# First attention of a two-block network: its four groups spread over four key/value projections instead of one group per projection

## The reference, cut to what matters

```python
def diff_attention(q1, q2, k1, k2, v, lam, bias_dist):     # per block of 128 queries
    def probs(q, k):
        s = einsum('bqhd,bkhd->bhqk', q, k) * scale + bias # q, k: 4 heads x 64
        s = where(causal, s, -inf)
        return softmax(s, axis=-1)
    a = probs(qa, k1) - lam * probs(qc, k2)
    return einsum('bhqk,bkhd->bqhd', a, v)                 # v: 4 heads x 128
...
    o = rms_norm(o, subln_g) * (1.0 - lambda_init)         # per head, over 128
    return concatenate([o, y], axis=-1) @ w_out
```

## Time and profile before

| | |
|---|---|
| median of 3 runs | 1134.58 us (1132.84 to 1136.03) |
| the profiled execution: its time | 1133.13 us |
| its span, first to last instruction | 1131.3 us |
| mean granted TensorE clock | 0.994 |
| PE matmul busy | 1099.1 us, 97% of the span |
| DVE / ACT / POOL busy | 701.5 / 517.9 / 65.0 us |
| HBM read | 222.95 MB, 198 GB/s over the span |

### The profile page before, as it was taken

How to read it: one execution, slowest core, us unless ns; L and a number is a source line. 1 busy time by engine, 2 the same in 40 slices (tenths; PEclk the granted TensorE clock), 3 DMA queues, 4 the chain that set the end, 5 groups by cost and what they waited for, 6 DMA issues and landing times.

```text
span 1131.3 us, 15644 instructions
## 1 busy us (share of the span) xinstructions
PE 1099.1 (97%) x6758; PEld 982.4 (87%) x6758; DVE 701.5 (62%) x666; ACT 517.9 (46%) x584; POOL 65.0 (6%) x116
## 2 busy tenths in 40 slices
PE   6998899999999999999999999999999998999998
PEld 4987689899989898998988898998788887898997
DVE  4655546468675767656645767668757467555544
ACT  5553544454344344333544544444655364453441
POOL 2200000010000000000001000000211010000000
PEclk9999899999999999999999999999999999999999
DMA  9834426264867756455535777586244463655531
GB/s 361 334 118 149 146 96 239 95 211 181 319 222 265 275 206 259 170 188 180 205 112 176 265 284 272 211 326 236 82 149 168 167 224 130 214 189 192 186 114 38
DMA packets 32356, 225.05 MB, mean 199 GB/s; under 512 B 3748, under 2 KB 4064, under 8 KB 7584
## 3 DMA queue, kind: packets, MB, share of 16 engines
q1 hardware_dynamic: 26640, 188.03, 45.8%
q0 software_dynamic: 5120, 34.85, 8.6%
q10 hardware_dynamic: 528, 1.16, 0.3%
HBM read 222.95 MB, written 1.08 MB: 198 GB/s over the span
## 4 chain that ended last, share of the span: by engine, by line
PE 89%; DVE 5%; ACT 3%; issue 1%; POOL 1%; DMA 0%; ACTq 0%; DVEq 0%; POOLq 0%
PE ps L485 46%; PE ps L470 37%; DVE lo L1504 2%; ACT hi L1044 1%; PE ps L545 1%; PE ps L705 1%; PE ps L726 1%; PE ps L880 0%; DMA h<-in_x 0%; PE ps L926 0%; DVE lo L1500 0%; DVE h L1541 0%; PE ps L682 0%; PE ps L666 0%; PE ps L859 0%
## 5 line engine op out<-in xcount | busy, mean ns | idle before, releaser
L1504 DVE TENSOR_TENSOR lo<-raw,hi 128x2048 fp32r<-128x2048 f32 x171 | 390.9, 2289 | 188.5 <-ACT hi L1044 188.3
L1044 ACT ACTIVATE hi<-raw 128x2048 fp32r<-128x2048 f32 x171 | 326.6, 1913 | 308.1 <-PE ps L485 164.2
L470 PE MATMUL ps<-xt_hi,hi 128*128 128x256 f32 x1088 | 308.9, 284 | 0.0
L470 PE MATMUL ps<-xt_lo,hi 128*128 128x256 f32 x1088 | 308.0, 283 | 0.0
L470 PE MATMUL ps<-xt_hi,lo 128*128 128x256 f32 x1088 | 308.0, 283 | 0.0
L485 PE MATMUL ps<-hi,yt_hi 128*128 128x512 f32 x544 | 214.1, 393 | 2.8 <-DVE yt_lo L1769 1.4
L485 PE MATMUL ps<-hi,yt_lo 128*128 128x512 f32 x544 | 212.5, 391 | 0.0
L485 PE MATMUL ps<-lo,yt_hi 128*128 128x512 f32 x544 | 212.5, 391 | 0.0
L470 PEld LDWEIGHTS ps<-xt_hi,hi 128*128 128x128 f32 x1088 | 208.9, 192 | 0.8 <-issue 0.2
L470 PEld LDWEIGHTS ps<-xt_hi,lo 128*128 128x128 f32 x1088 | 208.8, 192 | 0.8 <-issue 0.2
L470 PEld LDWEIGHTS ps<-xt_lo,hi 128*128 128x128 f32 x1088 | 208.8, 192 | 0.0
(11 more groups left out here) (261 smaller groups left out, 1053.6 us busy)
## 6 DMA issues: line engine op xcount, KB each, us to landing
raw<-in_weights SPq DMA_DIRECT2D x176, 1024.0 KB, 5.0
work<-in_w_ada POOLq DMA_DIRECT2D x16, 1536.0 KB, 7.2
work<-in_gains POOLq DMA_DIRECT2D x6, 512.0 KB, 4.1
work<-mod_rows POOLq DMA_DIRECT2D x6, 512.0 KB, 5.9
h<-in_x SPq DMA_DIRECT2D x2, 512.0 KB, 6.2
work<-in_gains ACTq DMA_DIRECT2D x2, 512.0 KB, 6.9
work<-in_mem POOLq DMA_DIRECT2D x2, 512.0 KB, 9.0
work<-in_pool SPq DMA_DIRECT2D x1, 1024.0 KB, 15.5
```

Source lines behind the costliest of these rows:

```text
L470: mm = pe.matmul(o, ws[:, slot, k, j * P:(j + 1) * P], xs[:, c, :], start=(c == 0 and n == 0 and j % 2 == 0), stop=(c == KC - 1 and n == 2 ...
L1044: act.activation(hi[:, p % RING], raw[:, p % RING], ACT.Copy).then_inc(hi_ready, 1)
L1504: dve.tensor_tensor(lo[:, p % RING], raw[:, p % RING], hi[:, p % RING].bitcast(F32), ALU.subtract)\
```

## The change

Nothing that is computed changes, and no size does. What changes is the order on PE, ACT and DVE between `l0_v` and `l0_out`. The three steps of a group become functions: `diff_scores(g)`, `diff_turn(g)`, `diff_values(g)` on PE, which are called as hooks inside the four key/value units; `diff_exps`, `diff_keep`, `diff_out` on ACT; `diff_logits`, `diff_probs` and `kept_one` (the eviction of a unit's second bank) on DVE. `head_sums` and `head_back` become hooks of `kv0 + 3`, and the output pair has none. PE:

```diff
-        for g in range(4):
-            ...                       (scores, unit kv0+g, turn, values)
-        pair(UNIT["l0_out"], ((yt_ready.at(("pool", 1)),), (yt_ready.at(("diff", 1)),)),
-             {(0, 0, 1): lambda: head_sums("d", one[:, :], diff_sq), (0, 1, 0): lambda: head_back("d")})
+        diff_scores(0)()
+        unit_w(kv0, MT, (0, 1), split("mem"), {(0, 2): diff_scores(1), (1, 1): diff_turn(0)})
+        unit_w(kv0 + 1, MT, (2, 3), hooks={(0, 0): diff_scores(2), (0, 1): diff_values(0), (0, 2): diff_turn(1),
+                                           (1, 0): diff_scores(3), (1, 1): diff_values(1), (1, 3): diff_turn(2)})
+        unit_x(kv0 + 2, MT, (0, 1), hooks={(0, 1): diff_turn(3), (0, 1, 2): diff_values(2), (1, 0): diff_values(3)})
+        unit_x(kv0 + 3, MT, (2, 3), hooks={(0, 1): lambda: head_sums("d", one[:, :], diff_sq),
+                                           (1, 0): lambda: head_back("d")})
+
+        pair(UNIT["l0_out"], ((yt_ready.at(("pool", 1)),), (yt_ready.at(("diff", 1)),)))
```

ACT (before: both splits behind `l0_v`, then per group the exponentials, `copy0` of the unit with its two splits, `keep_turned`, and the eviction of bank 7 after odd groups; then the square, the roots and the two `split_hi`):

```diff
+        refill(UNIT["l0_v"], 0)
+        diff_exps(0)
+        refill(UNIT["l0_v"], 1)
+        diff_exps(1)
+        diff_keep(0)
+        copy0(kv0, kv_k[:, 0:2, :])
+        diff_exps(2)
+        diff_keep(1)
+        diff_out(0)
+        refill(kv0 + 1, 0)
+        diff_exps(3)
+        diff_keep(2)
+        ...                           (eviction of bank 0 of kv0 + 1)
+        refill(kv0 + 1, 1)
+        diff_keep(3)
+        diff_out(1)
         ...
         act.activation(diff_sq, diff_o, ACT.Square).then_inc(*hsq.up("d"))
+        copy0(kv0 + 2, kv_v[:, 0, 0:NB])
         head_roots("d", 8, P)
         ...                           (split_hi of the normed attention, two of them)
+        copy0(kv0 + 3, kv_v[:, 0, NB:D])
```

DVE (before: both splits behind `l0_v` and the eviction, then per group logits, probabilities, eviction and splits; then the inverse, the norm, `split_lo`):

```diff
+        kept_one(UNIT["l0_v"], v_nat[:, 1, :])
+        diff_logits(0)
+        refill(UNIT["l0_v"], 0)
+        diff_probs(0)
+        refill(UNIT["l0_v"], 1)
+        diff_logits(1)
+        diff_probs(1)
+        refill(kv0, 0)
+        kept_one(kv0, kv_k[:, 2:4, :])
+        diff_logits(2)
+        diff_probs(2)
+        refill(kv0, 1)
+        diff_logits(3)
+        refill(kv0 + 1, 0)
+        diff_probs(3)
+        kept_one(kv0 + 1, kv_k[:, 6:8, :])
+        refill(kv0 + 1, 1)
+        refill(kv0 + 2, 0)
+        kept_one(kv0 + 2, kv_v[:, 1, 0:NB])
         head_inverse("d", 8)
+        refill(kv0 + 2, 1)
         head_norm("d", diff_o, [col("subln")])
         ...                           (split_lo, two of them)
+        refill(kv0 + 3, 0)
+        kept_one(kv0 + 3, kv_v[:, 1, NB:D])
+        refill(kv0 + 3, 1)
```

More of the change, by code:

```diff
@@ L658, in _ @@
         evicted(UNIT["l0_k"])
-        for g in range(4):
[L660 to L664, removed]
-                for a in range(2):
[L666 to L687, removed]
@@ L689, in _, with diff_scores, run @@
-        pair(UNIT["l0_out"], ((yt_ready.at(("pool", 1)),), (yt_ready.at(("diff", 1)),)),
-             {(0, 0, 1): lambda: head_sums("d", one[:, :], diff_sq), (0, 1, 0): lambda: head_back("d")})
+        def diff_scores(g):
+            def run():
+                hg, qt = g // 2, g % 2
+                nk = P * (qt + 1)
+                for s in range(2):
+                    o = claim(4 + s, ("s", ("d", g), s))
+                    r = slice(64 * s, 64 * s + 64)
+                    for a in range(2):
+                        mm = pe.matmul(o[:, a * S:a * S + nk], q_t[r, 2 * hg + a, qt * P:(qt + 1) * P],
+                                       k_t[r, 2 * hg + a, 0:nk], start=True, stop=True, skip_group_check=True)
+                    filled_by(mm, ("s", ("d", g), s))
+            return run
@@ new lines, in diff_turn, with run, diff_values @@
+        def diff_turn(g):
+            def run():
+                pe.wait_ge(*probs_ready.at(("d", g)))
+                turn_probs(("d", g), cut(hn[:, g % 2, 0:2 * S], 2), range(2), range(g % 2 + 1))
+            return run
+        def diff_values(g):
+            def run():
+                hg, qt = g // 2, g % 2
+                if g == 0:
+                    evicted(UNIT["l0_v"])
+                pe.wait_ge(*read(("t", ("d", g), 0)))
+                if qt == 0:
+                    claim(7, ("o", ("d", hg)))
+                for a in range(2):
+                    for kt in range(qt + 1):
+                        mm = pe.matmul(ps[:, 7, a * S + qt * P:a * S + (qt + 1) * P],
+                                       v_nat[:, kt, (2 * hg + a) * P:(2 * hg + a + 1) * P],
+                                       a_t[:, g % 2, a * (qt + 1) + kt, :],
+                                       start=(kt == 0), stop=(kt == qt), skip_group_check=True)
+                if qt == 1:
+                    filled_by(mm, ("o", ("d", hg)))
+            return run
@@ new lines, in _ @@
+        kv0 = UNIT["kv0"]
+        diff_scores(0)()
[5 more added lines that the diff above has]
+                                           (1, 0): lambda: head_back("d")})
@@ L1162, in _, with diff_exps @@
                      *read(label))
[L1163 to L1167, removed]
+        def diff_exps(g):
+            nk = P * (g % 2 + 1)
             e = hn[:, g % 2, :].rearrange("p (s a k) -> p s a k", s=2, a=2)
@@ L1175, in _, with diff_keep, diff_out @@
             ins.then_inc(*diff_exp.up(g))
[L1176 to L1183, removed]
+        def diff_keep(g):
+            keep_turned(("d", g), a_t[:, g % 2, 0:2 * (g % 2 + 1), :])
+        def diff_out(hg):
+            label = ("o", ("d", hg))
+            act.wait_ge(*fill(label))
+            act.activation(diff_o[:, 2 * hg:2 * hg + 2, :], cut(bank(label), 2), ACT.Copy).then_inc(*free(label))
+        kv0 = UNIT["kv0"]
+        refill(UNIT["l0_v"], 0)
[10 more added lines that the diff above has]
+        diff_keep(2)
+        act.wait_ge(*fill(("u", kv0 + 1, 0)))
+        act.activation(kv_k[:, 4:6, :], cut(bank(("u", kv0 + 1, 0)), 2), ACT.Copy).then_inc(*free(("u", kv0 + 1, 0)))
+        refill(kv0 + 1, 1)
+        diff_keep(3)
+        diff_out(1)
         act.wait_ge(*read(("o", ("d", 0))))
@@ L1646, in _, with diff_logits @@
             split_lo(("pool", b), part, pool_y[part])
-        copy1(UNIT["l0_v"], v_nat[:, 1, :])
         dve.wait_ge(*bias_masked.at(1))
         dve.wait_ge(*lam_ready.at(0))
-        for g in range(4):
+        def diff_logits(g):
             hg, qt = g // 2, g % 2
@@ L1657, in _ @@
                 dve.wait_ge(*fill(label))
+                if g >= 2 and s == 0:
+                    dve.wait_ge(*fill(("t", ("d", g - 2), 0)))
                 dve.scalar_tensor_tensor(e[:, s, :, 0:nk], cut(bank(label), 2)[:, :, 0:nk], 64.0 ** -0.5,
@@ L1664, in _, with diff_probs @@
                 .then_inc(*shift_ready.up(("d", g)))
-            u = UNIT["kv0"] + g
-            if g < 2:
-                refill(u, 0)
+        def diff_probs(g):
+            nk = P * (g % 2 + 1)
+            e = hn[:, g % 2, :].rearrange("p (s a k) -> p s a k", s=2, a=2)
             dve.wait_ge(*diff_exp.at(g))
@@ L1679, in _, with kept_one @@
             ins.then_inc(*probs_ready.up(("d", g)))
-            if g >= 2:
-                refill(u, 0)
+        def kept_one(u, dst):
             label = ("u", u, 1)
             dve.wait_ge(*fill(label))
[L1684 to L1688, removed]
+            src = bank(label)
+            dve.tensor_copy(dst, cut(src, 2) if len(dst.shape) == 3 else src).then_inc(*free(label))
+        kv0 = UNIT["kv0"]
+        kept_one(UNIT["l0_v"], v_nat[:, 1, :])
[17 more added lines that the diff above has]
+        kept_one(kv0 + 2, kv_v[:, 1, 0:NB])
         head_inverse("d", 8)
+        refill(kv0 + 2, 1)
         head_norm("d", diff_o, [col("subln")])
```

## The result

| | before | after |
|---|---|---|
| median | 1133.92 us (4 runs) | 1117.41 us (4 runs, 1116.20 to 1117.57) |
| profiled execution | 1133.13 us | 1117.57 us |
| span | 1131.3 us | 1115.7 us |
| from the scores of group 0 to `kv1a` | 93.98 us | 78.39 us |

The ratio is 0.9845, with a 95% interval of 0.9829 to 0.9862: 1.55% faster. (The two medians alone give 0.9854; on the same basis the two ways lie 1 us apart.) 0.9845 of the 1134.58 us of the text above is 1116.99, 2.5 us under my number and just outside the lower end of my range. So the direction and the mechanism held, and the gain was forecast too small. The change in the profiled execution, 15.56 us, is the change of the stage, 15.59: the stages behind moved as a whole.

The account below looks back on a forecast made before the run. PE, busy 97%, bounds the kernel. Idle 9.4 plus clock 5.1 gave 14.5 us, PE's remaining work 13.9; 1133.13 less 14.2 plus a 0.3 wait was put at 1119.0, raised to 1119.5 us, range 1117.0 to 1125.0.

Parts of the forecast that it names:

- the stages behind: Everything after the stage, from `kv1a` on, would shift earlier as a whole, neither longer nor shorter.
- A correction of 0.5 us upwards: From 1119.0 to 1119.5 us: a third of the 1.45 us by which the profiled execution lay under the median.
- the clock behind them: Three low-clock stretches following gaps in the stage would go, 1.7 us each, together 5.1 us.
- turn 3 is the tight place: Turn of group 3 on PE: DVE's probabilities only 0.3 us early; 0.3 us of waiting taken, bounds 0 and 1.5.
- ACT's three waits: ACT's queue held by `diff_out(0)`, `diff_out(1)` and the roots waiting for PE; the splits held up are needed only later.
- the layout: Step-by-step schedule of PE, DVE and ACT in the new order, with the output pair ending about 149.5 us, 150 with breaks.
- the four rivals: In us: clock stays low 1124.6, 0.14; queues late 1121.5 to 1125, 0.13; weight ring dry 1144, 0.03; gaps kept 1134, 0.03.
- Idle 9.4 us: PE's shown waits that would go: 6.2 us in front of the values and 3.2 us in front of the turns.
- What is left on PE, 80.1 us: PE's work remaining in the stage at full clock, 79.3 us plus 0.8 for breaks, against 93.98 before.
- 8 x 0.1 us for breaks: Hooks break PE's stream 14 times instead of 6; each further break costs 0.1 us, 0.8 us in all.
- The two sums: Gain in the stage counted twice: 14.5 us from idle time and clock, 13.9 us from PE's remaining work.
- The rule weighed: Transposes not counting as clock activity could bring a low stretch back in the hooks, up to 5.1 us; not followed.

Follow-up runs that it names:

- run 8: Kernel before, order untouched, with useless matmuls put into the gaps where PE stands idle around turns and values; 1128.29 us, stage 89.11 us.
- run 3: Changed kernel with the head sums and head back returned to the output pair; 1117.62 us, stage 78.39 us.
- Runs 4: Changed kernel with one PE wait added ahead of the output pair, for the split of half 18 (short gap); 1118.61 us.
- run 5: Changed kernel with one PE wait added ahead of the output pair, for the split of half 19 (long gap); 1123.87 us.
- run 6: Changed kernel with every matmul of the four turns and four values steps issued twice; 1120.98 us, stage 82.35 us.
- run 7: Changed kernel with hooks of turns and values put together, 11 breaks of the stream instead of 14; 1118.11 us, stage 78.38 us.
- runs 8 to 10: Useless matmuls in the kernel before's gaps, 1128.29 us; in two later gaps of the changed kernel, 1116.09 us; the changed kernel once more, 1117.72 us.
- run 2: Changed kernel with all its hooks, but ACT's and DVE's weight splits again ahead of the attention steps; 1123.61 us, stage 84.96 us.

## Why the prediction was right in kind and short in size

The step that failed is the size of the gain in the stage. I took 14.2 us, less 0.3 for a wait: the idle time at what the waits show (9.4 us, measured 10.7), and from the other side PE's remaining work at the rows' durations (80.1 us, measured 78.39). The stage gained 15.59. A correction of 0.5 us upwards at the end went the wrong way on top.

**Right.** That gaps and the clock behind them are the gain: 10.7 and 4.87 us (run 8), where I had 9.4 and 5.1. That the stages behind shift as a whole: 15.59 in the stage, 15.56 in the profiled execution. That PE doesn't wait, that turn 3 is the tight place, that ACT's three waits hold nothing that is needed: no wait in the stage, and the times of the layout within 0.5 us to the end. That moving the head sums changes nothing of PE's work: run 3. Of the four rivals none came: no low stretch and no wait in the stage, for `lo` or for anything else.

**Wrong, by terms:**
- *Idle 9.4 us.* I took what the waits show as what the gaps cost. Six gaps cost 10.7 us. Runs 4 and 5 show the reason in one gap: 0.16 us of the last matmul's tail in both, and 0.1 us of slow start in the short one, so six gaps lose 6 x 0.16 to 0.27 = 1.0 to 1.6 us more than is shown, and 1.3 are missing. The Trainium skill's first page, Trainium Kernel Development and Optimization, Performance Expectations, says that matmul busy time is a bad metric for how close a kernel is to its roofline, because matmuls are pipelined. The trace agrees that the overlap blurs such times, here on the side of idle time: 1.67 us shown, 1.96 us lost.
- *What is left on PE, 80.1 us.* It is 78.39. The turns at their busy time, 2.0, and the values measured ahead of a broken stream, 3.5, were 1.5 us too much: 1.3 and 2.65 (run 6). The 8 x 0.1 us for breaks isn't there for turns and values (run 7). (By the count that gives 6 before, there are 13 breaks after, not 14; the scores of group 0 stand in both.) 80.1 - 1.5 - 0.8 = 77.8. What is then short, 0.6 us, is at the scores and the head steps, where a break does cost: the matmul ahead of the scores at 84.65 takes 0.21 us to their start, and the first one behind 0.22, where a stream has 0.12. By distances of starts the whole stage closes: streams with their first matmuls 68.2, scores 3.45, turns 0.97, values 2.35, head steps 3.4, together 78.4 us.
- *Sum against layout.* The layout had turn prices of its own, 1.4 us for the four, and ended at 149.5, or 150 with breaks; the sum, with 2.0 us, ends at 70.85 + 80.1 = 150.95. The layout was the better one (149.22), and 93.98 - 79.15 = 14.8 us stood in it. I didn't compare them.
- *The last sum.* 1133.13 - 14.2 + 0.3 is 1119.2 and not 1119.0; done rightly the forecast would have been 0.2 us higher still.
- *The wait before turn 3, 0.3 us,* didn't come.
- *From the profiled execution to the median: 0.5 us added, the wrong way.* I let a third of the 1.45 us stay by which the profiled execution lay under the median. None did: after the change the median lies 0.16 us under the profiled execution. The scatter is a staircase: in the eleven runs of the kernel before that stood beside runs 8 to 10 the mean clock and the time go together, 0.995 with 1131.5 us, 0.994 with 1132.8 to 1133.4, 0.992 with 1134.5, 0.991 with 1135.8, 0.989 with 1136.8 to 1137.3. The profiled execution had four low stretches, three of them in the stage; by their mean clock others had fewer or more. The changed kernel's runs stand on 1.000 (1116.1 to 1116.2), 0.998 (1117.3 to 1117.8) and 0.996 (1118.9, whose trace has one stretch of 6.8 us). So removing gaps lowers the median at least as much as the profiled execution, and nothing was to be added.

The two sums, 14.5 and 13.9 us, erred to the same side; that they agreed said nothing of what both left out. The range's lower end, 1117.0, allowed for one error or for the luck of the later clock, not for both: 1133.1 - 15.6 - 1.4 for no low stretch at 780 us is 1116.1, which single runs reached.

**The rule weighed.** The Trainium skill, TensorE: Matmul & The Clock Gate, Part 4, says that transposes don't count as activity as matmuls do; by it the new hooks of transposes could have brought the low clock back. In the changed kernel twelve transposes lie in the stage at clock 1.00 throughout, in both profiled executions. They didn't bring it down; whether they count can't be told from a stage in which so little time is theirs. The rule stays open where transposes stand between gaps, as the eight at 780 us do; in run 5 the clock fell in a gap with no transpose in it. On the luck at the later places the trace agrees with the Trainium skill's same page, Part 1: at 780 us the low stretch came in some executions and not in others, behind the same instructions.

## What to carry to other kernels

Price a gap on TensorE by the distance of two matmul starts, not by the idle time shown, and a small step by what it takes when it is issued twice, or by the distance from its start to that of another small step behind it; both sums are then of one kind and can be checked against each other. Where two remedies shorten the same gaps (an order of queues, a pipeline by hooks), each alone can give well over half of what both give, here 9.6 and 9.0 of 15.6 us. Where a gap can't be removed, useless matmuls that fit into it win back what the clock would take, here 4.87 us of 93.98, and they can make the time steadier.

## What the runs showed of the hardware

- The clock fell behind gaps of 2.76 and 2.11 us, in one trace behind two of 0.7 us with small matmuls around them, and not behind 1.67 us (one trace) or 1.80 us (eleven traces, before at 941 us). Behind the same 1.95 us it fell in eight traces and not in three: the gap's length alone doesn't decide, and neither do the instructions.
- A low stretch lasted 3.4 us in most places. It lasted 6.8 us behind the 3.1 us wait of run 2, behind the 4.47 us gap of run 5 and once at 781 us in the changed kernel; where it began in a gap, PE worked for 5.5 to 6.2 us of it.
- Transposes and float matmuls of 128 columns take 0.11 us each from start to start when another small step follows (0.44 us for a row of four), though the mean duration of a transposition's row is 279 ns.
